# Differential attention scores from rounded parts and remainders, and the modulation's gate row in two parts

## The chip, the cores and the metric

The kernel runs on one core of a Trainium2 chip. The metric is the device time of one execution in microseconds (us), and lower is better. Six actors appear below: PE (TensorE, the matmuls; PEld are its weight loads), ACT (ScalarE), DVE (VectorE), POOL (GpSimd), SP (SyncE, which issues the DMAs here) and the DMA queues. Each engine works through its own instructions in order and waits on semaphores that the others raise.

## The reference, cut to what matters

Two layers run after one another on 1024 tokens of width 1024. The change lies in the second one, in its differential attention, and in a small product that makes the second layer's gate.

```python
# second layer, differential attention: 4 heads, each with two 64-wide halves m = 0, 1
scores_m = (q_m @ k_m.T) * 64 ** -0.5 + alibi_and_causal       # for m = 0, 1
p = softmax(scores_0) - lambda * softmax(scores_1)
o = rms_norm(p @ v) * (1 - lambda_init)                        # then a silu gate
# modulation: shift, scale, gate = split(silu(c) @ ada_w + ada_b)
```

All is float32. TensorE takes plain float32 operands, or operands that were rounded to the type fp32r. A product of full accuracy can also be made from rounded operands: each operand is split into a rounded part (HI) and a remainder (LO), and three products are added up, LO·HI + HI·LO + HI·HI (`PASSES`, line 73). The kernel does that already for all its big projections.

## The kernel before, in words

**The dense run of the second layer.** `Dense` (line 455) computes the projections of the second layer. It goes through *slots*. A slot is one 128x512 half of an output tile: 24 matmuls (8 pieces of depth times 3 passes) into one PSUM bank. The tile's weights are loaded raw, rounded by ACT (`split_high`, line 241) and their remainder is taken by DVE (`split_low`, line 252), one tile ahead. After a slot's matmuls ACT copies the bank to SBUF (a `MapTile`, line 361) and raises `free` for that bank. PE waits for `free` before it writes the same bank again. Slots are numbered from 0 to 51 here; slots 2n and 2n+1 are the two halves of tile n.

**Banks.** The slots 0 to 29 alternate between the banks 7 and 3 (`local`). From slot 30 on, all slots use bank 7 alone (`single`, line 3571), as banks 0 to 3 hold scores by then. So PE can begin slot s+1 only when bank 7 has been emptied of slot s. Slots 20 to 23 make k and q of head 0, slots 30 to 33 of head 1, slots 36 to 39 of head 2, slots 42 to 45 of head 3.

**Work beside the slots.** Other work is interleaved with the slots by hand. Sliding-window attention (`Attention`, scores on line 956, transposes on 967, products with v on 981) goes with the slots 21 to 30. Differential attention (`DiffAttention`, from line 2685) begins after slot 30. It has 32 units (4 heads, 8 blocks of 128 queries); a unit with n blocks of keys has the width 128 n, and n runs 1, 2, ..., 8 in the heads 0 and 2 and 8, ..., 1 in the heads 1 and 3. PE handles them in *bodies*: body u makes the scores of unit u (line 2777), the transposes of unit u-1 (line 2791) and the product with v of unit u-2 (line 2808). There is a body after every slot, and from slot 35 on another one in the middle of every odd slot, after 12 of its 24 matmuls.

**The chain of one unit.** When PE has scored unit u, DVE adds the distances and takes maxima (line 2898), ACT takes exponentials (line 2972), DVE weighs and joins the two halves (lines 2909 to 2913), and PE may then transpose unit u in body u+1.

**Order on DVE in a slot** (`Dense.vector`): first the work of the body in the middle of the slot, then the weights of the unit before (`early_dve`), then `split_low` if the slot is the tile's second half, then the tile's own `vector` (nothing for a `MapTile`), then the maxima of the body after the slot. `split_low` waits for ACT's `split_high`, which in its turn comes after ACT's copy of the slot.

**Row groups.** A score product has a depth of 64. The half m = 0 lies on the partitions 0 to 63 and m = 1 on 64 to 127, and a matmul with 64 rows takes one half of the array's rows. The profile shows a plain float32 matmul as two records of weight load and matmul, and an fp32r one as one.

**Modulation** (line 1795) runs beside the first layer. DVE accumulates silu(c)·ada_w into `acc`; at slot 19 of that run PE sums over the partitions: 16 products of one column (line 1846) and two products of 512 columns with a matrix of ones (line 1849), in plain float32.

## Time and profile before

| what | value |
|---|---|
| median of 3 runs | 1753.31 us (1753.15 to 1753.87) |
| the profiled execution | 1753.49 us, of which the span of its instructions is 1751.8 us |
| PE busy | 1722.8 us, 98% |
| DVE / ACT / POOL busy | 914.2 us (52%) / 653.5 us (37%) / 247.2 us (14%) |
| chain that ended last | 91% PE, 5% DVE, 2% ACT |
| granted TensorE clock | 0.997 of full speed |

The first part of the page says how long each engine had an instruction running, the fourth follows the work that ended last backwards from its end. The timeline of an engine groups neighbouring instructions of one line: start, duration of the group, engine, line, operation, tiles, shapes, count, and in brackets how long the engine had been idle and for whom. Where two groups follow each other closely, the difference of their starts is what the first one cost.

### The profile page before, as it was taken

To read this page: it belongs to the slowest core of one execution; us is meant where nothing else is said; L and a number is where in the kernel's file an instruction comes from. 1 tells how busy PE (TensorE), PEld (TensorE's weight loads), DVE (VectorE), ACT (ScalarE), POOL (GpSimd) and SP (SyncE) were. 2 spreads that over 40 slices of the span, in tenths; PEclk is the share of its full clock that TensorE was granted. 3 is DMA by queue.
4 is the path that set the end of the run, shared out by engine and by line. 5 is a ranking of instruction groups with operands and counts; after the bars stand their busy time and mean duration, and the time that the engine had idled before them with its cause. 6 is when DMAs were issued, how large, how long until landed. Compare 5 with 4: busy or idle time off the path is not lost.

```text
span 1751.8 us, 22440 instructions
## 1 busy us (share of the span) xinstructions
PE 1722.8 (98%) x8731; PEld 1397.1 (80%) x8731; DVE 914.2 (52%) x1529; ACT 653.5 (37%) x1225; POOL 247.2 (14%) x412
## 2 busy tenths in 40 slices
PE   7999999999999999999999999999999999999998
PEld 6788887778888888878888788888887777777786
DVE  5158878664436744863233222477242545757763
ACT  5234438621324433842113111323313453434731
POOL 3012210188901100000000000490000000000000
PEclk9999999999999999999999999999999999999999
DMA  4121110346232200211111211332703101001132
GB/s 146 50 78 41 44 37 2 119 141 196 85 123 72 61 25 28 79 34 50 50 54 39 88 43 30 109 132 79 162 25 101 47 25 37 25 25 49 43 128 107
DMA packets 148485, 122.94 MB, mean 70 GB/s; under 512 B 10572, under 2 KB 134043, under 8 KB 147739
## 3 DMA queue, kind: packets, MB, share of 16 engines
q1 hardware_dynamic: 148378, 121.49, 22.9%
q8 instruction: 70, 1.15, 0.3%
q14 instruction: 37, 0.30, 0.1%
HBM read 108.21 MB, written 13.26 MB: 69 GB/s over the span
## 4 chain that ended last, share of the span: by engine, by line
PE 91%; DVE 5%; ACT 2%; issue 2%; DMA 1%; SPq 0%; DVEq 0%; ACTq 0%
PE psum L91 59%; PE psum L309 8%; PE psum L79 7%; PE psum L981 2%; PE psum L956 2%; PE psum L2777 2%; PE psum L967 2%; PE psum L2808 2%; PE psum L2791 1%; PE psum L1790 1%; PE psum L781 1%; PE psum L1513 1%; ACT p L1085 1%; DVE roots L434 0%; PE psum L415 0%
## 5 line engine op out<-in xcount | busy, mean ns | idle before, releaser
L91 PE MATMUL psum<-hT,w_parts 128*128 128x512 f32 x3360 | 794.2, 392 | 4.0 <-ACT hT L690 2.4
L91 PEld LDWEIGHTS psum<-hT,w_parts 128*128 128x128 f32 x3360 | 627.3, 188 | 140.6 <-issue 5.5
L252 DVE TENSOR_TENSOR w_parts<-w_raw,w_parts 128x1024 fp32r<-128x1024 f32 x88 | 110.3, 1253 | 363.9 <-ACT w_parts L241 363.9
L91 PE MATMUL psum<-h2T,w_parts 128*128 128x512 f32 x1248 | 297.1, 394 | 0.0
L91 PEld LDWEIGHTS psum<-h2T,w_parts 128*128 128x128 f32 x1248 | 230.8, 188 | 48.3 <-issue 1.7
L1548 ACT ACTIVATE gate<-psum,cols 128x512 f32<-128x512 f32 x48 | 33.0, 688 | 284.3 <-PE psum L79 284.3
L79 PE MATMUL psum<-y_high,wp_parts 128*128 128x512 f32 x384 | 128.8, 395 | 0.3 <-DVE ya_low L1606 0.3
L241 ACT CAST w_parts<-w_raw 128x1024 fp32r<-128x1024 f32 x88 | 91.6, 1041 | 21.8 <-DMA w_raw<-w_in 17.2
L79 PEld LDWEIGHTS psum<-y_high,wp_parts 128*128 128x128 f32 x384 | 72.0, 188 | 18.8 <-DVE ya_low L1606 1.6
L309 PE MATMUL psum<-w_parts,y_parts 128*128 128x512 f32 x360 | 82.6, 390 | 0.6 <-DVE w_parts L302 0.6
L434 DVE RECIPROCAL x<-x 128x512 f32<-128x512 f32 x24 | 80.3, 3344 | 0.0
L2972 ACT ACTIVATE diff_p<-diff_p,diff_small 128x128 f32<-128x128 f32 (+7 forms) x64 | 49.2, 770 | 81.1 <-DVE diff_small L2902 81.1
L309 PEld LDWEIGHTS psum<-w_parts,y_parts 128*128 128x128 f32 x360 | 67.3, 188 | 15.1 <-DVE w_parts L302 1.0
L309 PE MATMUL psum<-w_parts,merged_high 128*128 128x512 f32 x240 | 75.9, 392 | 0.0
L1560 DVE TENSOR_TENSOR gate<-psum,gate 128x512 f32<-128x512 f32 x32 | 22.0, 688 | 80.5 <-ACT gate L1548 80.5
L2898 DVE CUSTOM_DVE_ANT_0 diff_p<-psum,far 128x128 f32<-128x128 f32 (+7 forms) x64 | 45.8, 754 | 27.2 <-PE psum L2777 27.0
L2086 POOL MEMSET ssm_cos<- 128x16 f32 x1 | 0.1, 127 | 403.8 <-PE psum L79 403.8
L405 POOL TENSOR_TENSOR sq_parts<-x,sq_parts 128x512 fp32r<-128x512 f32 x24 | 31.0, 1293 | 176.4 <-ACT sq_parts L398 176.4
L309 PEld LDWEIGHTS psum<-w_parts,merged_high 128*128 128x128 f32 x240 | 45.1, 188 | 10.0
L248 DVE TENSOR_TENSOR w_parts<-w_raw,w_parts 128x512 fp32r<-128x512 f32 x32 | 24.5, 792 | 47.2 <-ACT w_parts L237 46.9
L309 PE MATMUL psum<-w_parts,merged_low 128*128 128x512 f32 x112 | 44.0, 393 | 0.0
L1085 ACT ACTIVATE p<-p,att_small 128x128 f32<-128x128 f32 (+1 forms) x96 | 42.1, 439 | 1.9 <-DVE att_small L1023 0.9
(378 smaller groups left out, 2271.2 us busy)
## 6 DMA issues: line engine op xcount, KB each, us to landing
w_raw<-w_in SPq DMA_DIRECT2D x188, 256.0 KB, 3.4
middle_a<-ada_w SPq DMA_DIRECT2D x32, 384.0 KB, 3.8
w_raw<-w_out SPq DMA_DIRECT2D x16, 512.0 KB, 3.8
qkT<-x SPq DMA_DIRECT2D x8, 512.0 KB, 7.0
w_raw<-m_w_kv SPq DMA_DIRECT2D x16, 256.0 KB, 3.2
base<-x SPq DMA_DIRECT2D x8, 512.0 KB, 4.0
x_kept<-x_ring SPq DMA_DIRECT2D x8, 512.0 KB, 3.4
base<-x_kept SPq DMA_DIRECT2D x8, 512.0 KB, 3.5
```

Of the source, the lines that this page charges most:

```text
L79: last = pe.matmul(out, lhs(a, k), rhs(b, k), start=(k == 0 and n == 0), stop=(k == depth - 1 and n == 2))
L91: last = pe.matmul(out, lhs(a, k), rhs(b, k), start=(n == 0), stop=(n == len(SLOT) - 1))
L241: act.copy(self.parts[:, u, HI, :, :], self.raw[:, :, :]).then_inc(self.high, 2)
L252: dve.tensor_tensor(self.parts[:, u, LO, :, :], self.raw[:, :, :], self.parts[:, u, HI, :, :].bitcast(F32), ALU.subtract).then_inc(self.lo ...
L309: last = pe.matmul(out, lhs(a, k), self.part(b, k)[:, c0:c0 + width], start=(i == 0 and n == 0), stop=(i == KT - 1 and n == 2))
L434: dve.reciprocal(rs, rs).then_inc(run.inverted, 1)
L956: last = pe.matmul(self.S_(u)[:, h, 0:d["width"]], d["q"][h], d["k"][h], start=True, stop=True)
L967: last = pe.transpose(self.T_()[:, (2 * h + b) * P:(2 * h + b + 1) * P], self.p[u % self.ring][:, h, b * P:(b + 1) * P], self.ident)
L981: last = pe.matmul(d["out"](h, self.O_(u)), d["values"](h, b), self.pT[u % self.turns][:, (2 * h + b) * P:(2 * h + b + 1) * P], start=(b = ...
L1085: last = act.activation(into, src, ACT.Exp, bias=self.negative[:, s, h:h + 1], accum_out=sums[:, h:h + 1])
L2898: last = dve.tensor_tensor_reduce(self.p[:, s, m, 0:width], bank(self.core, 2 * m)[:, 0:width], self.far[:, D - width:D], 2.0 ** -(5 + h), ...
L2972: last = act.activation(self.p[:, s, m, 0:width], self.p[:, s, m, 0:width], ACT.Exp, bias=self.negative[:, s, m:m + 1], accum_out=self.tot ...
```

## The change

1. q and k of the differential attention are kept as two fp32r parts. Their tiles become `PartsTile`s: ACT writes the rounded part (times the scale), then DVE computes bank·scale − rounded part as one `scalar_tensor_tensor` of 128x512, and DVE, no longer ACT, raises `free`.
2. The scores take three fp32r passes per half m and per chunk of at most 512 columns in place of one plain float32 product.
3. Modulation's gate row: ACT rounds `acc_gate`, DVE takes the remainder in place (both at slot 18), and PE sums both parts with fp32r ones, which the run's head tiles have made already (`same`), in four matmuls in place of two.
4. `diff_q` and `diff_k` take 16 KB more per partition, so the tiles behind them and two of the output norm's tiles move up by 16 KB, and the scratch space for dynamic DMAs is set to 256 bytes to make room.

```diff
+class PartsTile(GateTile):
+    def scalar(self, act, run, s):
+        slot = run.slots[s]
+        wait = self.wait and self.wait(slot.h)
+        if wait:
+            act.wait_ge(*wait)
+        act.activation(self.high(slot.h), run.out(s), ACT.Copy, scale=self.scale).then_inc(run.mapped, 1)
+
+    def vector(self, dve, run, s):
+        slot = run.slots[s]
+        dve.wait_ge(run.mapped, run.gates.index(s) + 1)
+        dve.scalar_tensor_tensor(out=self.low(slot.h), in0=run.out(s), scalar=self.scale,
+                                 in1=self.high(slot.h).bitcast(F32), op0=ALU.mult,
+                                 op1=ALU.subtract).then_inc(run.free[slot.bank], 1)
...
@@ Modulation
+        if s == self.SUM_AT - 1:
+            act.wait_ge(self.weighed, 4 * KT)
+            act.copy(self.high, self.acc_gate).then_inc(self.round_made, 1)
...
+            pe.wait_ge(self.same_made(), 1)
+            pe.wait_ge(self.rest_made, 1)
             for h in range(2):
-                last = pe.matmul(bank(self.core, 5 + h, 1), self.ones,
-                                 self.acc[:, 2 * D + h * HALF:2 * D + (h + 1) * HALF], start=True, stop=True)
+                half = slice(h * HALF, (h + 1) * HALF)
+                pe.matmul(bank(self.core, 5 + h, 1), self.same, self.high[:, half], start=True, stop=False)
+                last = pe.matmul(bank(self.core, 5 + h, 1), self.same, self.low[:, half], start=False, stop=True)
...
+        if s == self.SUM_AT - 1:
+            dve.wait_ge(self.round_made, 1)
+            dve.tensor_tensor(self.low, self.acc_gate, self.high.bitcast(F32), ALU.subtract).then_inc(self.rest_made, 1)
...
@@ DiffAttention.scores
         for c0 in range(0, width, HALF):
             cw = min(HALF, width - c0)
-            for m in range(2):
-                rows = slice(64 * m, 64 * m + 64)
-                last = pe.matmul(bank(self.core, 2 * m)[:, c0:c0 + cw], self.qT[rows, h % 2, t * P:(t + 1) * P],
-                                 self.kT[rows, h % 2, c0:c0 + cw], start=True, stop=True)
+            for n, (a, b) in enumerate(PASSES):
+                for m in range(2):
+                    rows = slice(64 * m, 64 * m + 64)
+                    last = pe.matmul(bank(self.core, 2 * m)[:, c0:c0 + cw], self.qT[rows, h % 2, a, t * P:(t + 1) * P],
+                                     self.kT[rows, h % 2, b, c0:c0 + cw], start=(n == 0), stop=(n == 2))
...
-            qT = core.sb(run_stack, "diff_q", [P, 2, S])
-            kT = core.sb(run_stack, "diff_k", [P, 2, S])
+            qT = core.sb(run_stack, "diff_q", [P, 2, 2, S], F32R)
+            kT = core.sb(run_stack, "diff_k", [P, 2, 2, S], F32R)
...
-                return [MapTile(at(1024, h), ACT.Copy, lambda m: half(kT[:, h % 2, :], m), **where),
-                        MapTile(at(512, h), ACT.Copy, lambda m: half(qT[:, h % 2, :], m),
-                                scale=64 ** -0.5 * 2.0 ** (5 + h), **where),
+                part = lambda a, n: (lambda m: half(a[:, h % 2, n, :], m))
+                return [PartsTile(at(1024, h), part(kT, HI), part(kT, LO), **where),
+                        PartsTile(at(512, h), part(qT, HI), part(qT, LO), scale=64 ** -0.5 * 2.0 ** (5 + h), **where),
...
-    nc = bacc.Bacc("TRN2", target_bir_lowering=False, num_devices=1)
+    nc = bacc.Bacc("TRN2", target_bir_lowering=False, num_devices=1, dynamic_dma_scratch_size=256)
```

On PE, around the bodies 1 and 2 (after the slots 31 and 32), the rows stand before as here (a row is line, operation, output and inputs, shape of the output, count; L2777 are scores, L2791 transposes, L2808 the product with v, L91 a slot):

```order
L2777 MATMUL psum<-diff_k,diff_q 128x256 x2
L2791 MATMUL psum<-const,diff_p 128x128
L91 MATMUL psum<-h2T,w_parts 128x512 x24
L2777 MATMUL psum<-diff_k,diff_q 128x384 x2
L2791 MATMUL psum<-const,diff_p 128x128 x2
```

and with the change, where the lines 2812 and 2826 are the scores and the transposes:

```order
L2812 MATMUL psum<-diff_k,diff_q 128x256 x6
L2826 MATMUL psum<-const,diff_p 128x128
L91 MATMUL psum<-h2T,w_parts 128x512 x24
L2812 MATMUL psum<-diff_k,diff_q 128x384 x6
L2826 MATMUL psum<-const,diff_p 128x128 x2
```

Nothing has moved on PE; each pair of score matmuls has become six.

On DVE, in slot 31 (the second half of head 1's k) and up to the weights of its unit, before (L252 is `split_low`, the ISA rows are the maxima):

```order
L252 TENSOR_TENSOR w_parts<-w_raw,w_parts 128x1024
L2898 ISA diff_p,diff_small<-psum,far 128x256
L2898 ISA diff_small 128x1
L2898 ISA diff_p,diff_small<-psum,far 128x256
L2898 ISA diff_small 128x1
```

and with the change:

```order
L252 TENSOR_TENSOR w_parts<-w_raw,w_parts 128x1024
L398 SCALAR_TENSOR_TENSOR diff_k<-psum,diff_k 128x512
L2933 ISA diff_p,diff_small<-psum,far 128x256
L2933 ISA diff_small 128x1
L2933 ISA diff_p,diff_small<-psum,far 128x256
```

The remainder stands behind `split_low` and ahead of the maxima, and bank 7 is free only after it. All the second halves (slots 21, 23, 31, 33, 37, 39, 43, 45) look like this.

On DVE, in slot 36 (the first half of head 2's k), before (L1531 puts turned v rows away):

```order
L2913 SCALAR_TENSOR_TENSOR diff_p<-diff_p,diff_small 128x896
L1531 COPY diff_v<-psum 128x512
L2898 ISA diff_p,diff_small<-psum,far 128x1024
L2898 ISA diff_small 128x1
L2898 ISA diff_p,diff_small<-psum,far 128x1024
```

and with the change:

```order
L2948 SCALAR_TENSOR_TENSOR diff_p<-diff_p,diff_small 128x896
L1553 COPY diff_v<-psum 128x512
L398 SCALAR_TENSOR_TENSOR diff_k<-psum,diff_k 128x512
L2933 ISA diff_p,diff_small<-psum,far 128x1024
L2933 ISA diff_small 128x1
```

The remainder of a first half stands directly ahead of the maxima of the body after the slot. In slot 36 it waits for an ACT copy which itself waits until unit 7, the last of head 0, has been scored, since head 2's k takes the place of head 0's.

## Rows read from the trace of the kernel before

**Rows 1.** The page, part 1: busy us (share of the span) xinstructions of each engine.

```profile
PE 1722.8 (98%) x8731; PEld 1397.1 (80%) x8731; DVE 914.2 (52%) x1529; ACT 653.5 (37%) x1225; POOL 247.2 (14%) x412
```

**Rows 2.** Groups by form: line, engine, operation, names, shapes, count, busy us, mean ns.

```profile
L91 PE MATMUL psum<-memT,w_parts 128*128 128x256 f32 x192 | 23.9, 280 | 0.4 <-DVE mergedT L436 0.3
...
L2884 DVE SCALAR_TENSOR_TENSOR yT<-psum,diff_norm,yT 128x512 f32<-128x512 f32 x8 | 5.6, 746 | 0.7 <-PE psum L2758 0.7
```

**Rows 3.** Timeline of PE, score bodies with n = 1 and n = 8.

```profile
1439.30 0.49 PE L2777 MATMUL psum<-diff_k,diff_q 64*128 64x128 f32 x4
1439.72 5.75 PE L91 MATMUL psum<-h2T,w_parts 128*128 128x512 f32 x24
...
1487.36 1.99 PE L2777 MATMUL psum<-diff_k,diff_q 64*128 64x512 f32 x8
1489.28 0.98 PE L2791 MATMUL psum<-const,diff_p 128*128 128x128 f32 x7
```

**Rows 4.** Timeline of PE, other matmuls with few rows or few columns.

```profile
57.86 2.10 PE L839 MATMUL psum<-mergedT 33*4 33x384 f32 x6
...
447.76 2.37 PE L1846 MATMUL psum<-const,middle_a 128*128 128x1 f32 x20
449.99 1.96 PE L1849 MATMUL psum<-middle_a,const 128*128 128x512 f32 x4
...
1404.28 1.14 PE L956 MATMUL psum<-wk,wq 64*128 64x256 f32 x8
1405.35 1.09 PE L967 MATMUL psum<-const,swa_p 128*128 128x128 f32 x8
```

**Rows 5.** Timeline of ACT in the slots 31, 32 and 36.

```profile
1445.51 0.60 ACT L361 ACTIVATE diff_k<-psum 128x512 f32<-128x512 f32 x1 [3.93 <-PE psum L91]
1446.00 1.04 ACT L241 CAST w_parts<-w_raw 128x1024 fp32r<-128x1024 f32 x1
...
1452.01 0.60 ACT L361 ACTIVATE diff_q<-psum 128x512 f32<-128x512 f32 x1 [1.47 <-PE psum L91]
...
1489.46 0.60 ACT L361 ACTIVATE diff_k<-psum 128x512 f32<-128x512 f32 x1 [4.21 <-PE psum L2777]
```

**Rows 6.** Timeline of DVE, `split_low` in the slots 31, 33, 39, 43 and 45.

```profile
1447.14 1.23 DVE L252 TENSOR_TENSOR w_parts<-w_raw,w_parts 128x1024 fp32r<-128x1024 f32 x1 [4.67 <-ACT w_parts L241]
...
1460.54 1.23 DVE L252 TENSOR_TENSOR w_parts<-w_raw,w_parts 128x1024 fp32r<-128x1024 f32 x1 [3.92 <-ACT w_parts L241]
...
1526.71 1.23 DVE L252 TENSOR_TENSOR w_parts<-w_raw,w_parts 128x1024 fp32r<-128x1024 f32 x1 [0.57 <-ACT w_parts L241]
...
1562.66 1.23 DVE L252 TENSOR_TENSOR w_parts<-w_raw,w_parts 128x1024 fp32r<-128x1024 f32 x1 [1.73 <-ACT w_parts L241]
...
1579.57 1.23 DVE L252 TENSOR_TENSOR w_parts<-w_raw,w_parts 128x1024 fp32r<-128x1024 f32 x1 [0.65 <-ACT w_parts L241]
```

**Rows 7.** Timeline of PE, the matmuls of the next slot after 31, 32, 33, 39, 43, 45.

```profile
1446.25 5.72 PE L91 MATMUL psum<-h2T,w_parts 128*128 128x512 f32 x24
...
1453.17 5.70 PE L91 MATMUL psum<-h2T,w_parts 128*128 128x512 f32 x24
...
1460.61 5.71 PE L91 MATMUL psum<-h2T,w_parts 128*128 128x512 f32 x24
...
1528.05 5.70 PE L91 MATMUL psum<-h2T,w_parts 128*128 128x512 f32 x24
...
1562.19 5.70 PE L91 MATMUL psum<-h2T,w_parts 128*128 128x512 f32 x24
...
1580.74 5.71 PE L91 MATMUL psum<-h2T,w_parts 128*128 128x512 f32 x24
```

**Rows 8.** Timelines of DVE and PE: maxima and transposes of unit 7.

```profile
1489.40 1.22 DVE L2898 CUSTOM_DVE_ANT_0 diff_p<-psum,far 128x1024 f32<-128x1024 f32 x1 [1.24 <-PE psum L2777]
...
1496.27 1.09 PE L2791 MATMUL psum<-const,diff_p 128*128 128x128 f32 x8
```

**Rows 9.** Timeline of PE: transposes of the window attention's unit 0, after slot 22.

```profile
1371.41 0.66 PE L967 MATMUL psum<-const,swa_p 128*128 128x128 f32 x4
```

25 lines of the change are left out of this document (17 added, 8 removed).

## The prediction

> **What bounds the kernel now.** I read the page's busy times first: PE has an instruction running in 98% of the span [rows 1], so the time changes with what PE executes and with every wait that PE gets. Then I read PE's timeline from slot 30 to the end of the dense run, and beside it those of ACT and DVE, since the change gives DVE new work there. Two things are to be seen. A score body costs its matmuls plus a fixed part. And PE's stretch between two slots is short (0.85 us after slot 31: ACT's copy begins at 1445.51 [rows 5], the next slot at 1446.25 [rows 7]); in it bank 7 must be emptied. A copy of 0.60 us on ACT alone just fits.
>
> **Part 1, the scores.** With n = 1 a body's scores take 1439.72 − 1439.30 = 0.42 us, with n = 8 1489.28 − 1487.36 = 1.92 us [rows 3]: 0.21 + 0.214 n. The slope is 4 columns' time at 2.4 GHz per column of one half m (128 × 4 / 2.4 GHz = 213 ns), so the two halves run side by side. That this comes from the two row groups is seen from two other rows: three plain float32 products that all lie in the first row group take 2.0 us for 384 columns each (six records of 0.32 us, one after another), while four products of 256 columns, two in each group, take 1.07 us, half of what they would one by one, plus 0.21 [rows 4]. The 0.21 us is thus the price of going to 64 rows and back. Over 4 heads and n = 1 to 8 the scores cost 4 × (8 × 0.21 + 36 × 0.214) = 37.5 us.
>
> With the change a chunk takes three passes. No row shows an fp32r matmul of 64 rows. What a pass costs is read from fp32r matmuls of full depth: 24 in 5.7 us, 0.235 us for 512 columns [rows 3, 7], and 23.9 / 192 = 0.125 us for 256 [rows 2], so about 0.02 us beyond the columns. For 128 columns the weight load is the floor: 20 records with one column each lie 2.23 / 20 = 0.11 us apart [rows 4]. I take the two halves as parallel, as they are now, and keep 0.21 us for the switch. Then a unit costs 0.54, 0.59, 0.75, 0.92, 1.25, 1.29, 1.46, 1.62 us for n = 1 to 8 (from n = 5 on it has two chunks), 8.42 us a head and 33.7 in all: **−3.8 us**. It is a small gain since three passes replace four columns' time, and weight loads eat part of it.
>
> The bounds: 23.0 us if passes run at column rate with no switch and no load exposed; 60.7 us if the halves run one after another (53.9 for passes, 6.7 for switches). I choose the parallel value, as its nearest row is the same body in plain float32. The Trainium skill (TensorE: Matmul & The Clock Gate, Part 3, on packing small matmuls) measures four row tiles at 3.07 times, 77% of the ideal; by that as an estimate passes would take 27 / 0.77 = 35 us and the sum would be some 6 us worse after waits. The float32 rows reach the full factor of two, so the sum doesn't use it.
>
> **Part 2, the remainder on DVE before bank 7 is free.** The new instruction reads PSUM and SBUF, 128x512; the nearest row is the `scalar_tensor_tensor` of the same form, 0.75 us long and 0.70 us of DVE's time (5.6 / 8) [rows 2]. The ends are 0.62 and 0.75. In a *second half* DVE does `split_low` first, which waits for ACT's copy and ACT's rounding of the weights. Bank 7 is free 0.75 us after `split_low` gives DVE up (1.14 us after its start) and PE sees it 0.07 us later. The scores ahead are shorter by the amounts of part 1.
> - Slot 31: 1447.14 + 1.14 + 0.82 = 1449.10 [rows 6]; PE would begin at 1446.25 − 0.05 [rows 7]: **2.9 us** of waiting.
> - Slot 33: 1460.54 + 1.96 = 1462.50, against 1460.61 − 0.15: **2.0**.
> - Slot 39: 1526.71 + 1.96 = 1528.67, against 1528.05 − 0.15: **0.8**.
> - Slot 43: 1562.66 + 1.96 = 1564.62, against 1562.19 − 0.10: **2.5**.
> - Slot 45: 1579.57 + 1.96 = 1581.53, against 1580.74 − 0.20: **1.0** [rows 6, 7].
> - Slot 37: nothing. Its body holds scores with n = 7, eight transposes and a product of eight, more than 4 us, and the bank needs some 3.9.
>
> In a *first half* there is no `split_low`: copy 0.60, hand-over 0.10, remainder 0.75, hand-over 0.07, so 1.52 us after the copy begins. Slot 32: 1452.01 + 1.52 = 1453.53 [rows 5] against 1453.17 − 0.10 [rows 7]: 0.45. The slots 30 and 42 miss by about 0.1 each, 44 is even, 36 and 38 have bodies of over 4 us. **0.6 us** together. What is queued on DVE behind the waiting remainder are the maxima of the body after the slot. In the slots with a wait on PE the unit's chain then has PE's whole next slot (5.7 us) as cover.
>
> **Part 3, the maxima of unit 7 come late.** In slot 36 ACT's copy begins only at 1489.46 [rows 5], when unit 7 is scored; the maxima of unit 7 begin at 1489.40 now [rows 8] and would stand behind the remainder, at 1489.46 + 0.60 + 0.08 + 0.70 = 1490.84, 1.44 us later. This chain (maxima, exponentials, weights over 1024 columns) takes until 1496.27, when PE transposes [rows 8]; PE's scores of the next unit end there too, so nothing hides it. With these scores 0.29 us shorter the wait is **1.7 us**.
>
> **Part 4, window attention.** In slot 21 the remainder stands behind `split_low` and ahead of the maxima of its unit 0, whose transposes are already the thing PE waits for at 1371.41 [rows 9]. 0.70 us later: **0.7 us**. The later units have over 1 us to spare. Elsewhere in the run two banks alternate, and a remainder has a whole slot of cover.
>
> **Part 5, gains given back.** At units 11, 22, 25 and 29 and in the last four bodies PE meets a chain of DVE and ACT that is just in time or late; scores that end sooner only wait longer there: **0.5 us** of the 3.8.
>
> **Part 6, the gate row.** Two plain products (four records, 1.8 us without the tail of the last [rows 4]) become four fp32r matmuls of 0.235 us: **−0.85 us**. ACT's rounding (1.04 us, as that of the weights [rows 5]) and DVE's remainder (1.23 us by the form of `split_low`) lie in slot 18, over 3 us ahead of use. Moved addresses and the smaller scratch: every DMA stays in its place on SP; nothing.
>
> **The sum.** Waits 2.9 + 2.0 + 0.8 + 2.5 + 1.0 + 0.6 + 1.7 + 0.7 + 0.5 = 12.7 us; less 3.8 and 0.85: +8.05 us on the profiled execution's 1753.49 (span 1751.8 and 1.7 around it), 1761.5. The median lies 0.2 us below that execution: **1761.3 us**, 0.46% slower.
>
> **The rivals.**
> *A: the two halves don't overlap in fp32r.* For it: no row shows it overlapping. Against: rows 3 and 4, where the row group decides and not the operand. The scores cost 60.7 us, +23.2; each body then covers more, and the waits fall to about 7 (slots 31, 33 and 43 keep 5.8 of 7.4, window attention 0.7, the rest nearly nothing): 1753.3 + 23.2 + 7 − 0.85 = 1782.7.
> *B, the other side: the passes run at column rate.* If going to 64 rows cost nothing in fp32r and the loads hid wholly, the scores would take 23.0 us, −14.5. The waits on bank 7 and on late chains would grow to about 16.5, as every body is shorter by the same amount that PE then stands: 1753.3 − 14.5 + 17.3 (with window attention's 0.7) − 0.85 = 1755.3, within 0.2% of before. It decides from scores under 25 us on. Against it: the 0.21 us appears in every body of 64 rows, whatever n.
> *C: the waits don't come*, since the remainder is not on the way of bank 7, or `split_low` isn't ahead of it: 1753.3 − 3.8 − 0.85 + 2 = 1750.6. Against: the order on DVE and the single bank are written in the program.
> *D: weight loads of the two halves go one after another*, 0.21 us a pass as a floor: 39.1 us of scores, +1.6 instead of −3.8, part of which replaces waits: 1765. It is in my own range.
>
> **How the numbers follow.** The forecast goes from 1757 (switch at half its price, remainder of 0.62 us) over D's 1765 to passes half as dear again (40.5 us for 27, +13.5, of which about 5 replaces waits), 1769: 0.80. A 0.12, B 0.05, C 0.03. The range takes in the forecast and B's bound, 1755.3 to 1769; A stays out with its 0.12. A measurement of this kernel tells 0.2% (3.5 us) from no change. Slower by more: forecast and A, less a little for a low forecast, 0.90. Same: B and that little, 0.07. Faster: C, 0.03.
>
> **What the changed profile would show.** Score bodies: 0.54 us with n = 1, 1.62 with n = 8 (A: 3.0; B: 1.3). Idle time of PE ahead of line 91, released by DVE's line 398: near 2.9, 2.0, 0.8, 2.5, 1.0 us after the slots 31, 33, 39, 43 and 45. A wait of some 1.7 us ahead of the transposes of unit 7. PE's busy time would fall while the span grows. If the bodies are right and the waits are absent, parts 2 to 4 are wrong; if the waits are there and the bodies are long, part 1 is.

## The result and the profile after

| what | before | changed kernel |
|---|---|---|
| median | 1753.54 us (4 runs beside the changed kernel) | 1763.6 us (1762.81 to 1764.69, 4 runs) |
| ratio to before | 1 | 1.0056 (95% interval 1.0044 to 1.0068) |
| the profiled execution, its span | 1753.49 us, 1751.8 us | 1764.33 us, 1762.5 us |
| mean granted TensorE clock | 0.997 | 0.994 |

The change makes the kernel 0.56% slower. Predicted were 1761.3 us and a range of 1755.3 to 1769.0.

The page of the changed kernel, the busy times of part 1 and the chain by engine of part 4:

```profile
PE 1723.5 (98%) x8827; PEld 1408.4 (80%) x8827; DVE 924.6 (52%) x1546; ACT 655.3 (37%) x1226; POOL 250.5 (14%) x412
...
PE 91%; DVE 5%; ACT 2%; issue 2%; DMA 0%; ACTq 0%; DVEq 0%
```

Against [rows 1] PE is busy 0.7 us more, while the prediction had its busy time fall, as its scores became shorter. That was the first sign of something that the prediction doesn't have.

PE's timeline, the score bodies with n = 1 and n = 8 (start, duration of the group, engine, line, operation, tiles, shapes, count, and in brackets the idle time and its releaser), to be held against [rows 3]:

```profile
1440.01 0.55 PE L2812 MATMUL psum<-diff_k,diff_q 64*128 64x128 f32 x6
1440.49 0.73 PE L91 MATMUL psum<-h2T,w_parts 128*128 128x512 f32 x2
...
1494.10 1.66 PE L2812 MATMUL psum<-diff_k,diff_q 64*128 64x512 f32 x12
1495.69 0.98 PE L2826 MATMUL psum<-const,diff_p 128*128 128x128 f32 x7
```

From start to start the scores take 0.48 us with n = 1 and 1.59 with n = 8. Between them are 0.55, 0.72, 0.90, 1.18, 1.25 and 1.42 us: 8.09 us a head, 32.4 in all, against 37.5 before.

PE's timeline, the next slot after 31, 32, 33, 39, 43 and 45, to be held against [rows 7]:

```profile
1449.87 7.33 PE L91 MATMUL psum<-h2T,w_parts 128*128 128x512 f32 x24 [2.84 <-DVE diff_k L398]
1458.61 5.74 PE L91 MATMUL psum<-h2T,w_parts 128*128 128x512 f32 x24
1467.99 5.68 PE L91 MATMUL psum<-h2T,w_parts 128*128 128x512 f32 x24 [1.82 <-DVE diff_q L398]
...
1535.71 5.72 PE L91 MATMUL psum<-h2T,w_parts 128*128 128x512 f32 x24 [0.38 <-DVE diff_q L398]
...
1572.16 7.30 PE L91 MATMUL psum<-h2T,w_parts 128*128 128x512 f32 x24 [2.33 <-DVE diff_k L398]
...
1592.88 5.70 PE L91 MATMUL psum<-h2T,w_parts 128*128 128x512 f32 x24 [0.81 <-DVE diff_q L398]
```

Two things are to be seen. Five of the six have PE idle ahead of them, released by DVE's line 398, the remainder; before, none had. And two of them last 7.3 us for the same 24 matmuls that take 5.7 us elsewhere. PE's clock at these places, in windows of 2 us (window, length, then busy us and instructions of PE, PEld, DVE, ACT and POOL, the granted clock, the DMA share, GB/s):

```profile
1450.00:1452.00 2.00, 2.00 (x6) 1.54 (x7) 0.77 (x7) 1.24 (x5) 0.00 (x0) 0.50 0.77 226
...
1468.00:1470.00 2.00, 2.00 (x9) 1.68 (x10) 1.69 (x7) 0.70 (x2) 0.00 (x0) 1.00 0.72 210
...
1574.00:1576.00 2.00, 2.00 (x6) 1.51 (x6) 1.05 (x3) 0.65 (x3) 0.00 (x0) 0.50 0.26 77
```

Behind the waits of 2.84 and 2.33 us PE ran at 0.50, that is at 1.2 GHz, and did six matmuls in 2 us instead of nine; behind the one of 1.82 us it ran at 2.4 GHz. The half clock counts as busy time: at these two slots alone it adds 3.2 us of it, against some 5 us that the scores save.

How slot 31 goes, in the timelines of ACT and DVE (against [rows 5, 6]):

```profile
1446.26 0.60 ACT L393 ACTIVATE diff_k<-psum 128x512 fp32r<-128x512 f32 x1 [3.92 <-PE psum L91]
```

```profile
1447.89 1.22 DVE L252 TENSOR_TENSOR w_parts<-w_raw,w_parts 128x1024 fp32r<-128x1024 f32 x1 [4.66 <-ACT w_parts L241]
1449.04 0.68 DVE L398 SCALAR_TENSOR_TENSOR diff_k<-psum,diff_k 128x512 fp32r<-128x512 f32 x1
```

The copy is done by 1446.9. The remainder could start then, but DVE's queue has `split_low` first, and this waits for ACT's rounding. The remainder runs from 1449.04, PE goes on at 1449.87.

Unit 7 and window attention: DVE's timeline in slot 36, then PE's ahead of the transposes of unit 7 and around slot 22 (against [rows 8, 9]):

```profile
1496.50 0.69 DVE L398 SCALAR_TENSOR_TENSOR diff_k<-psum,diff_k 128x512 fp32r<-128x512 f32 x1 [1.60 <-ACT diff_k L393]
1497.11 1.21 DVE L2933 CUSTOM_DVE_ANT_0 diff_p<-psum,far 128x1024 f32<-128x1024 f32 x1
```

```profile
1503.97 1.09 PE L2826 MATMUL psum<-const,diff_p 128*128 128x128 f32 x8 [1.61 <-DVE diff_p L2948]
```

```profile
1370.88 1.14 PE L978 MATMUL psum<-wk,wq 64*128 64x256 f32 x8 [0.54 <-ACT swa_p L1107]
```

The wait of unit 7 is where it was forecast. That of window attention stands one step earlier: PE waits 0.54 us ahead of the next unit's scores (line 978, before 956) for ACT's exponentials, and not ahead of the transposes. The trace of before has no idle time at these scores.

### The profile page after: what moved, and what is told of

The parts are those of the page before. It is cut to its first block, busy times and chain, and to the rows that moved or that the text cites. A ratio compares the mean times of both kernels' runs of the same rounds, so it can differ in the third digit from the quotient of the medians.

```text
span 1762.5 us, 22654 instructions
## 1 busy us (share of the span) xinstructions
PE 1723.5 (98%) x8827; PEld 1408.4 (80%) x8827; DVE 924.6 (52%) x1546; ACT 655.3 (37%) x1226; POOL 250.5 (14%) x412
## 4 chain that ended last, share of the span: by engine, by line
PE 91%; DVE 5%; ACT 2%; issue 2%; DMA 0%; ACTq 0%; DVEq 0%
PE psum L91 58%; PE psum L309 10%; PE psum L79 7%; PE psum L978 2%; PE psum L1003 2%; PE psum L989 2%; PE psum L2843 1%; PE psum L2812 1%; PE psum L1812 1%; PE psum L2826 1%; PE psum L1535 1%; ACT w_parts L241 1%; DVE roots L456 0%; PE psum L803 0%; PE psum L437 0%
## 5 line engine op out<-in xcount | busy, mean ns | idle before, releaser
L91 PE MATMUL psum<-hT,w_parts 128*128 128x512 f32 x3360 | 795.3, 393 | 4.1 <-ACT hT L712 3.1
L91 PEld LDWEIGHTS psum<-hT,w_parts 128*128 128x128 f32 x3360 | 628.7, 189 | 140.5 <-issue 4.4
L91 PE MATMUL psum<-h2T,w_parts 128*128 128x512 f32 x1248 | 300.3, 397 | 8.3 <-DVE diff_k L398 5.2
L252 DVE TENSOR_TENSOR w_parts<-w_raw,w_parts 128x1024 fp32r<-128x1024 f32 x88 | 111.2, 1264 | 358.4 <-ACT w_parts L241 358.3
L91 PEld LDWEIGHTS psum<-h2T,w_parts 128*128 128x128 f32 x1248 | 233.1, 190 | 58.4 <-issue 10.7
L446 ACT ACTIVATE x<-psum,const 128x512 f32<-128x512 f32 x24 | 16.5, 689 | 70.2 <-PE psum L438 70.2
```

What stands on the lines that cost most here:

```text
L91: last = pe.matmul(out, lhs(a, k), rhs(b, k), start=(n == 0), stop=(n == len(SLOT) - 1))
L252: dve.tensor_tensor(self.parts[:, u, LO, :, :], self.raw[:, :, :], self.parts[:, u, HI, :, :].bitcast(F32), ALU.subtract).then_inc(self.lo ...
```

## Experiments on the eviction

**DVE takes the remainder first** (e1_remainder_first).

```diff
+            parts = isinstance(self.tiles[slot.n], PartsTile)
+            if parts:
+                self.tiles[slot.n].vector(dve, self, s)
             if slot.last and slot.n + 2 < len(self.tiles):
                 w.split_low(dve, slot.n // 2 + 1, slot.n % 2)
...
-            self.tiles[slot.n].vector(dve, self, s)
+            if not parts:
+                self.tiles[slot.n].vector(dve, self, s)
```

> The changed kernel with one thing else: in a slot of k or q DVE takes the remainder (line 398) ahead of split_low instead of behind it. Theory: what makes PE stand after the slots 31, 33, 39, 43 and 45 is that bank 7 is freed behind split_low. Then the waits fall from 2.84, 1.82, 0.38, 2.33, 0.81 us to about 0.6, 0, 0, 0.4, 0.1, -7.1 us together. If the half clock that PE shows after the two longest waits comes from these waits, its 2 x 1.6 us go too: 1763.6 - 7.1 - 3.2 = 1753.3 us. Rival 1, the clock fell for another reason in these stretches: 1756.5. Rival 2, the bank's release isn't what PE waits for: 1763 and the same waits.

Measured: 1753.87 us (1751.46 to 1755.66, 11 runs), ratio to before 0.9996 (0.9987 to 1.0005). PE's timeline has two waits for line 398 left, and both slots behind them are at full clock:

```profile
1446.12 5.72 PE L91 MATMUL psum<-h2T,w_parts 128*128 128x512 f32 x24 [0.70 <-DVE diff_k L398]
...
1562.04 5.72 PE L91 MATMUL psum<-h2T,w_parts 128*128 128x512 f32 x24 [0.20 <-DVE diff_k L398]
```

One exchange of two instructions on DVE takes away all that the change had cost, some 10 us in the medians. Set beside the changed kernel, start by start, e1 gains 11.1 us from 1370 to 1593 us: 1.6 at each of the two slots that were at half clock, the rest where the waits were. The theory holds, half clock included; both rivals fall.

**The scores alone** (e2_scores_alone), on the kernel before:

```diff
-            for m in range(2):
-                rows = slice(64 * m, 64 * m + 64)
-                last = pe.matmul(bank(self.core, 2 * m)[:, c0:c0 + cw], self.qT[rows, h % 2, t * P:(t + 1) * P],
-                                 self.kT[rows, h % 2, c0:c0 + cw], start=True, stop=True)
+            for n in range(3):
+                for m in range(2):
+                    rows = slice(64 * m, 64 * m + 64)
+                    last = pe.matmul(bank(self.core, 2 * m)[:, c0:c0 + cw], self.qT[rows, h % 2, t * P:(t + 1) * P],
+                                     self.kT[rows, h % 2, c0:c0 + cw], start=(n == 0), stop=(n == 2))
...
-            qT = core.sb(run_stack, "diff_q", [P, 2, S])
+            qT = core.sb(run_stack, "diff_q", [P, 2, S], F32R)
```

> The kernel before, with nothing but the scores changed: ACT writes k and q as fp32r, and each score product is made three times from these same parts (the remainders are left out, so the scores are three times what they should be), with six matmuls a chunk as in the changed kernel. Eviction, order on DVE and gate row are as before. Theory: the bodies' scores cost 32.4 instead of 37.5 us, -5.1, of which about 0.5 comes back at late chains of DVE: 1753.5 - 4.6 = 1748.9 us. Rival: bodies that end sooner only wait longer for DVE and ACT, so little is left: 1752 to 1753.5. Score bodies of 0.48 us with n = 1 and 1.59 with n = 8 in either case.

Measured: 1750.48 us (1748.70 to 1751.88, 11 runs), ratio 0.9979 (0.9970 to 0.9987), 3.3 us less than before beside it. The bodies take 0.48 and 1.59 us, as expected. From 1440 us to the end the trace gains 4.0 us on that of before, so 1.1 of the 5.1 came back as waits, not 0.5, and the median lies between the theory's 1748.9 us and the rival's 1752. No slot has a wait for an eviction. So the scores by themselves are a gain, and it is the eviction that turns the sign.

**The remainder alone** (e3_remainder_alone), on the changed kernel, with the gate row undone too:

```diff
-            for n, (a, b) in enumerate(PASSES):
-                for m in range(2):
-                    rows = slice(64 * m, 64 * m + 64)
...
+            for m in range(2):
+                rows = slice(64 * m, 64 * m + 64)
+                last = pe.matmul(bank(self.core, 2 * m)[:, c0:c0 + cw],
+                                 self.qT[rows, h % 2, HI, t * P:(t + 1) * P].bitcast(F32),
+                                 self.kT[rows, h % 2, HI, c0:c0 + cw].bitcast(F32), start=True, stop=True)
```

> The changed kernel with the scores and the gate row undone: k and q are evicted in two parts (ACT, then DVE behind split_low), but the scores are one plain float32 product of the rounded part (the remainder is left out of them), and the gate row is two plain products. Theory: the waits stay, a little smaller since the bodies ahead are as long as before: 2.8, 1.65, 0.3, 2.2, 0.7 and 0.25 us for slots 31, 33, 39, 43, 45, 32, unit 7 late by 1.4, window attention 0.7: +10.0; with the half clock after the two longest waits +3.2 more: 1766.7 us. Rival 1, without half clock: 1763.5. Rival 2, the waits come from shorter score bodies and not from the eviction: under 1756.

Measured: 1767.7 us (1766.86 to 1769.86, 4 runs), ratio 1.0081 (1.0068 to 1.0095). PE's timeline after the slots 31 and 43:

```profile
1450.84 7.24 PE L91 MATMUL psum<-h2T,w_parts 128*128 128x512 f32 x24 [2.75 <-DVE diff_k L398]
...
1574.92 5.68 PE L91 MATMUL psum<-h2T,w_parts 128*128 128x512 f32 x24 [2.20 <-DVE diff_k L398]
```

The waits are there without the new scores, at the sizes expected (2.75, 1.66, 0.39, 2.20, 0.56 us; 1.27 at unit 7). Only one of the two half clocks came. The median is still 1 us above the expectation. The profiled execution has 1.1 us of difference to that of before already ahead of 1370 us, with a half clock from 266 us on and another at 450 us, on which more below. Whether the other three executions had them isn't known.

**A raw copy frees the bank** (e6_raw_copy), on the changed kernel:

```diff
     def scalar(self, act, run, s):
...
-        act.activation(self.high(slot.h), run.out(s), ACT.Copy, scale=self.scale).then_inc(run.mapped, 1)
+        act.activation(self.raw(slot.h), run.out(s), ACT.Copy,
+                       scale=self.scale).then_inc(run.free[slot.bank], 1)
+
+    def round(self, act, run, s):
+        slot = run.slots[s]
+        act.wait_ge(run.free[slot.bank], slot.prior + 1)
+        act.copy(self.high(slot.h), self.raw(slot.h)).then_inc(run.mapped, 1)
...
+    def rest(self, dve, run, s):
+        slot = run.slots[s]
+        dve.wait_ge(run.mapped, run.gates.index(s) + 1)
+        dve.tensor_tensor(self.low(slot.h), self.raw(slot.h), self.high(slot.h).bitcast(F32),
+                          ALU.subtract).then_inc(run.rested, 1)
```

`raw` is the place of `low`, seen as float32. `round` is called behind `split_high`, `rest` behind the maxima of the body after the slot.

> The changed kernel with another eviction of k and q: ACT copies the bank, scaled and unrounded, into the place of the remainder, and this copy alone raises free (as before the change); behind split_high ACT rounds from there, and DVE subtracts in place, behind the maxima of the body after the slot. Theory: bank 7 is free as early as in the kernel before, no maxima stand behind a remainder, so all of the waits after slots, that of unit 7 (1.6 us) and that of window attention (0.5 us) go, and the scores keep their -5.1 less about 0.5: the time of e2_scores_alone, 1750.0 us, a score body of 1.59 us with n = 8, no wait for line 398 on PE. Rival: ACT's additional 0.5 us a slot ahead of the exponentials comes out in waits ahead of PE's transposes: 1752 us.

Measured: 1750.16 us (1748.56 to 1751.65, 10 runs), ratio 0.9974 (0.9965 to 0.9983). On another chip, as e13_raw_copy_again:

> e6_raw_copy once more, beside the two kernels that differ from it at the modulation alone: 1750.2 us, 0.9974 of the kernel before, if the gain of e6 holds on another chip.

Measured: 1751.02 us (1749.30 to 1753.92, 11 runs), ratio 0.9980 (0.9971 to 0.9989). In the trace of e6 ACT copies and rounds in slot 31, PE starts the next slot at once, and the transposes of unit 7 wait 0.33 us instead of 1.61:

```profile
1446.24 0.60 ACT L394 ACTIVATE diff_k_raw<-psum 128x512 f32<-128x512 f32 x1 [3.73 <-PE psum L91]
1446.74 1.04 ACT L241 CAST w_parts<-w_raw 128x1024 fp32r<-128x1024 f32 x1
1447.67 0.62 ACT L400 CAST diff_k<-diff_k_raw 128x512 fp32r<-128x512 f32 x1
```

```profile
1446.98 1.39 PE L91 MATMUL psum<-h2T,w_parts 128*128 128x512 f32 x5
```

```profile
1495.79 1.09 PE L2840 MATMUL psum<-const,diff_p 128*128 128x128 f32 x8 [0.33 <-DVE diff_p L2962]
```

```profile
1449.90 0.69 DVE L408 TENSOR_TENSOR diff_k<-diff_k_raw,diff_k 128x512 fp32r<-128x512 f32 x1
```

No wait for an eviction is left on PE. DVE's remainder costs the same 0.6 us as before, but nobody waits for it; ACT's additional rounding doesn't show either. This version computes all of the change and is faster than both kernels: 3 to 4 us less than the kernel before, about 13 less than the changed one.

## Experiments on the half clock behind a wait

**The bank held longer** (e7_bank_held), on e1:

```diff
+        for n in range(5 if slot.bank == 7 and slot.last and s >= 30 else 1):
+            if n:
+                run.repeats += 1
+                last.then_inc(run.repeated, 1)
+                dve.wait_ge(run.repeated, run.repeats)
+            last = dve.scalar_tensor_tensor(out=self.low(slot.h), in0=run.out(s), scalar=self.scale,
+                                            in1=self.high(slot.h).bitcast(F32), op0=ALU.mult, op1=ALU.subtract)
+        last.then_inc(run.free[slot.bank], 1)
```

> e1_remainder_first, but in the slots 31, 33, 37, 39, 43 and 45 DVE writes the remainder five times, so that bank 7 is free some 2.7 us later. It measures what a wait on PE does to the clock behind it. From the waits 0.70 and 0.20 us of e1 and those of the changed kernel, PE should stand 3.4 us after slot 31, 2.4 after 33, 0.95 after 39, 2.9 after 43 and 1.4 after 45. Theory: the half clock follows a long wait (2.84, 2.75 and 2.33 us had it behind them so far, 2.20, 1.82 and 1.66 had not), so the slots behind the waits of 3.4, 2.9 and 2.4 us take 7.2 us instead of 5.7, the two others 5.7. Rival: the half clock comes at its own times and has nothing to do with the wait: 5.7 us behind one of the long ones or 7.2 behind a short one. Time about 1753.9 + 11 + 4.5 = 1769.

Measured: 1770.5 us (one run). PE's timeline after the slots 31, 33, 39 and 43:

```profile
1451.37 7.31 PE L91 MATMUL psum<-h2T,w_parts 128*128 128x512 f32 x24 [3.60 <-DVE diff_k L403]
1470.23 5.72 PE L91 MATMUL psum<-h2T,w_parts 128*128 128x512 f32 x24 [2.59 <-DVE diff_q L403]
...
1540.29 5.71 PE L91 MATMUL psum<-h2T,w_parts 128*128 128x512 f32 x24 [1.49 <-DVE diff_q L403]
1577.48 7.28 PE L91 MATMUL psum<-h2T,w_parts 128*128 128x512 f32 x24 [3.10 <-DVE diff_k L403]
```

The waits of 3.60 and 3.10 us have a slot of 7.3 us behind them, that of 2.59 us has not, although the theory wanted it behind all three. After slot 45, 1.80 us, there is none either. So a longer wait does bring the half clock on, at two places that had none in e1, but not every long wait does: the theory holds in part, and the rival's sign, full speed behind one of the long waits, was seen too. The time is 1.5 us above the expected 1769.

**The halves in a row** (e8_halves_in_a_row), on the changed kernel:

```diff
-            for n, (a, b) in enumerate(PASSES):
-                for m in range(2):
-                    rows = slice(64 * m, 64 * m + 64)
+            for m in range(2):
+                rows = slice(64 * m, 64 * m + 64)
+                for n, (a, b) in enumerate(PASSES):
```

> The changed kernel with the six score matmuls of a chunk in another order: three passes of half m = 0, then three of m = 1, in place of m = 0 and m = 1 by turns. Theory: two matmuls run side by side only if they follow each other directly and lie in different row groups, so within a half the passes run one after another and only one of the five transitions overlaps: with n = 8 a body's scores take 2 x 5 x 0.213 + 0.2 = 2.3 to 2.8 us instead of 1.59, all scores some 50 us instead of 32.4, and the time is about 1778 us, less what takes the place of waits (3 to 5 us), so 1773 to 1778. Rival: the hardware overlaps the two halves whatever the order, or they never ran side by side: 1.6 us and the same time as the changed kernel, 1763.6.

Measured: 1768.92 us (one run). What it says of the scores stands in the next section. Of the waits it shows this:

```profile
1451.54 8.52 PE L91 MATMUL psum<-h2T,w_parts 128*128 128x512 f32 x24 [2.83 <-DVE diff_k L398]
1470.86 7.31 PE L91 MATMUL psum<-h2T,w_parts 128*128 128x512 f32 x24 [1.82 <-DVE diff_q L398]
```

The waits are those of the changed kernel, 2.83 and 1.82 us, yet here the second has the half clock behind it as well, and behind the first it lasted longer, 2.8 us lost instead of 1.6. With 2.33 us after slot 43 the third came too. In this trace that is 2.8 us more than in the changed kernel's; the rest of its 4.6 us lies ahead of 1440 us.

So, over the slots of the five traces with such waits (the changed kernel, e1, e3, e7, e8): 3.60, 3.10, 2.84, 2.83, 2.75 and two waits of 2.33 us had the half clock behind them, 2.59, 2.20, 1.80, 1.66, 1.49 and less had not, and 1.82 us once had and once had not. Seven of the nine waits of over 2 us had it behind them, and one of the shorter ones. The length alone doesn't decide between 1.8 and 2.6 us. What else does is open. The Trainium skill (TensorE: Matmul & The Clock Gate, Part 1, What's actually happening) says that a monitor of the engine's recent activity sets the clock to one of two levels and that it runs freely, not in step with the kernel. The traces agree as far as they go: only 0.50 and 1.00 and mixtures of them show, and equal waits end differently.

The traces have a better sample of equal waits than the slots. In the first layer PE waits 1.82 us for DVE at 265 to 267 us in all fourteen traces. In six of them (the changed kernel, e3, e5, e6, e8, e10) the half clock begins within 1.6 us of the end of this wait, in the other eight, that of before among them, it doesn't come. In PE's timeline of the changed kernel and of before, the same eight matmuls:

```profile
265.66 2.09 PE L978 MATMUL psum<-qkT 64*128 64x256 f32 x8 [1.82 <-DVE att_small L1045]
```

```profile
266.69 1.14 PE L956 MATMUL psum<-qkT 64*128 64x256 f32 x8 [1.82 <-DVE att_small L1023]
```

Here it cost the changed kernel 0.95 us against before. e5, which has nothing of the new eviction, has the half clock here too, and e1, which has the eviction, has not, so nothing speaks for this 0.95 us being the change's doing.

## Experiments on the row groups

In e8, the body of unit 7 in PE's timeline:

```profile
1498.64 1.66 PE L2812 MATMUL psum<-diff_k,diff_q 64*128 64x512 f32 x12
1500.23 0.98 PE L2826 MATMUL psum<-const,diff_p 128*128 128x128 f32 x7
```

1.59 us, as in the changed kernel, and so it is for every n. My theory, that two matmuls overlap only if they follow each other in the program, is refuted. Either the halves run side by side in whatever order, or the gain isn't from the row groups.

**Both halves in one row group** (e10_same_rows), on e6:

```diff
                     rows = slice(64 * m, 64 * m + 64)
+                    rows = slice(0, 64)
```

> e6_raw_copy, but all six score matmuls of a chunk take their operands from the partitions 0 to 63, so half m = 1 is computed from the data of m = 0 and the output is not the reference's. Everything else is as in e6. Theory: two matmuls run side by side because they lie in different row groups, in whatever order they are issued; in one row group they run one after another: with n = 8 a body's scores take 12 x 0.213 + 0.2 = 2.8 us instead of 1.58, the scores about 54 us in place of 32, and the time is 1750.2 + 21 = 1771. Rival: the side by side comes from something else (the depth of 64, the two banks): 1.6 us and 1750.

Measured: 1771.84 us (one run). The body of unit 7:

```profile
1490.89 3.01 PE L2827 MATMUL psum<-diff_k,diff_q 64*128 64x512 f32 x12
1493.83 0.87 PE L2841 MATMUL psum<-const,diff_p 128*128 128x128 f32 x6
```

2.94 us instead of 1.59; over n = 1 to 8 the bodies take 0.81, 0.90, 1.26, 1.59, 2.20, 2.30, 2.64 and 2.94 us, 58.6 in all instead of 32.3. It is the row groups. These 58.6 us are also what rival A had priced at 60.7, and 1771 was hit within a microsecond, since nearly nothing waits in this kernel. The Trainium skill (TensorEngine Tiling (Array Packing), Tiling Modes, Key Properties) says that different tiles of the array can execute loads and matmuls in parallel. The two runs agree: 58.6 / 32.3 is a factor of 1.81, and e8 shows it in another order of issue too.

## Experiments on the gate row

The profiled pair shows the opposite of what I had forecast here. PE's timeline of the kernel before, behind the two plain products of [rows 4]:

```profile
451.39 6.01 PE L91 MATMUL psum<-hT,w_parts 128*128 128x512 f32 x24
457.24 1.03 PE L1451 MATMUL psum<-const,middle_b 128*128 128x128 f32 x8
```

and of the changed kernel, with the granted clock of that window:

```profile
449.90 0.77 PE L1880 MATMUL psum<-gate_high,same 128*128 128x512 f32 x1
450.46 0.63 PE L1881 MATMUL psum<-gate_low,same 128*128 128x512 f32 x1
...
451.74 6.39 PE L91 MATMUL psum<-hT,w_parts 128*128 128x512 f32 x24
457.97 1.03 PE L1473 MATMUL psum<-const,middle_b 128*128 128x128 f32 x8
```

```profile
450.00:452.00 2.00, 2.00 (x6) 1.63 (x6) 0.01 (x1) 1.97 (x3) 1.77 (x4) 0.50 0.50 143
```

From the first gate matmul to line 1451 (now 1473) it was 7.25 us (449.99 to 457.24) and is 8.07 (449.90 to 457.97): +0.8 instead of −0.85. The matmuls stand 0.43 us apart and not 0.235.

**The gate row alone** (e5_gate_row_alone), on the kernel before, with the change's own lines in `Modulation` and nothing else of it.

> The kernel before with nothing but the gate row changed: rounded part and remainder at slot 18, four fp32r matmuls at slot 19. Theory 1: the four matmuls take 0.235 us each in place of 0.43, -0.85 us: 1752.7 us. Theory 2, from the trace of the changed kernel, where the granted clock was 0.50 from 450 to 452 us and these matmuls stood 0.43 us apart: the clock falls here and the slot behind starts slow, +0.8: 1754.3 us, with a granted clock of about one half in the 2 us behind the sixteen products of one column.

Measured: 1754.23 us (1751.97 to 1755.15, 11 runs), ratio 1.0002 (0.9993 to 1.0011). Clock 0.50 from 450 to 452 us, 7.97 us for the stretch: theory 2, as far as the profiled run goes. The times can't tell the two theories apart: the interval runs from −1.2 to +1.9 us and takes in both −0.85 and +0.8.

**The four matmuls first** (e9_gate_first), on e5:

```diff
-            for j in range(2 * KT):
-                pe.matmul(bank(self.core, 4, 1)[:, j:j + 1], self.acc[:, j * P:(j + 1) * P],
-                          self.ones[:, 0:1], start=True, stop=True)
...
+            for j in range(2 * KT):
+                last = pe.matmul(bank(self.core, 4, 1)[:, j:j + 1], self.acc[:, j * P:(j + 1) * P],
+                                 self.ones[:, 0:1], start=True, stop=True)
             last.then_inc(self.summed, 1)
```

> e5_gate_row_alone, but with the four gate matmuls ahead of the sixteen products of one column instead of behind them. Theory: it is the sixteen products that the half clock follows. Then the four gate matmuls take 0.235 us each at full clock, and the half clock falls on the slot behind: this slot takes 1.7 us longer, and the time is that of e5, 1754.2 us. Rival 1: with the gate row out of the half clock the time is 0.9 us shorter, 1753.3. Rival 2: the half clock starts ahead of the products and has another cause: the gate matmuls stay 0.43 us apart here too.

Measured: 1754.83 us (1750.60 to 1757.24, 11 runs), ratio 1.0000 (0.9991 to 1.0009). The gate matmuls were 0.24 us apart, at full clock; the products and the slot behind them paid instead, 4.54 us for the products (3.5 at full clock) and 7.72 for the slot:

```profile
446.19 4.68 PE L1858 MATMUL psum<-const,middle_a 128*128 128x1 f32 x32
450.73 7.88 PE L91 MATMUL psum<-hT,w_parts 128*128 128x512 f32 x24
```

So in this trace the half clock began within the sixteen products of one column and stayed for the slot behind them. From the first of these twenty matmuls to line 1451 it took 13.2 us (445.25 to 458.45), against 10.0 in e13 below, whose clock was full (446.81 to 456.80): 3.2 us lost, where I had expected 1.7. The theory holds as to the place, not as to the size, and both rivals fall in this trace.

**The products in three pieces** (e11_columns_spread), on e6:

```diff
...
+    def tensor_lows(self, pe, s):
+        self.columns(pe, s, 0, 5)
+
+    def tensor_mid(self, pe, s):
+        self.columns(pe, s, 5, 10)
+
     def tensor(self, pe, s):
+        self.columns(pe, s, 10, 2 * KT)
```

> e6_raw_copy, but the sixteen products of one column of the modulation stand at three places of slot 19 (five after its eighth matmul, five after its twelfth, six at its end) instead of together at its end. Theory: the half clock at 450 us follows 3.5 us of one-column products in one piece. In pieces of 1.1 to 1.3 us they don't bring it on, the four gate matmuls take 0.235 us each and the slot behind runs at full clock: 1.7 us less than e6, 1748.5 us. Rival: the half clock comes all the same: 1750.2.

Measured: 1749.23 us (1748.12 to 1751.44, 5 runs), ratio 0.9968 (0.9956 to 0.9981), whose interval overlaps those of e6. In its trace the half clock came earlier, behind the first two pieces, and the twelve matmuls of the slot behind these took 4.4 us (444.42 to 448.85). The gate matmuls were at full clock:

```profile
446.00:448.00 2.00, 2.00 (x6) 1.60 (x5) 0.00 (x0) 0.00 (x0) 1.76 (x4) 0.50 0.00 0
```

The theory that pieces don't bring it on is refuted; whether the spreading gains half a microsecond can't be told from five runs.

**The gate row undone** (e12_gate_row_undone), on e6: the gate's lines as in the kernel before.

> e6_raw_copy with the gate row as in the kernel before (two plain float32 products). It gives the gate row's own worth. As I predicted it (four fp32r matmuls at 0.235 us instead of 1.8 us) this kernel should be 0.85 us slower than e6, 1751.0. Against that stands that the half clock falls at this place: where it does, the plain products cost twice as much as well (449.99 to 453.37 us in the trace of e2_scores_alone), so these runs should be some 2.5 us above those of e6, and where it doesn't, 0 to 0.9 above: a median of 1750.5 to 1752.5 and a wider spread.

Measured: 1749.75 us (1749.27 to 1751.74, 7 runs), ratio 0.9973 (0.9962 to 0.9984), beside 1751.02 us (0.9980) for e13 on the same chip. The expected median of 1750.5 to 1752.5 was missed: this kernel is not slower than e6. With this kernel the gate row in two parts is worth nothing that these runs can tell.

What it would be worth at an equal clock the traces do say. In e13 the clock was 1.00 here, as in the trace of before:

```profile
450.30 0.48 PE L1894 MATMUL psum<-gate_high,same 128*128 128x512 f32 x1
...
456.80 1.04 PE L1487 MATMUL psum<-const,middle_b 128*128 128x128 f32 x8
```

At full clock the stretch takes 6.50 us in the new form and 7.25 in the old, −0.75, close to the −0.85 of the prediction. With the half clock it depends on how long this lasts. In the new form the stretch takes 8.0 to 8.1 us in six traces and 9.1 in e7 (449.42 to 458.50), where the half clock lasted twice as long as in these (0.54, 0.50, 0.50 and 0.75 in the windows of 2 us from 448 to 456 us, against 0.98, 0.50, 0.67 and 1.00 in the changed kernel); in the old form it takes 8.9 in e3 (450.68 to 459.61) and 10.1 in e12 and e2 (448.74 to 458.82, 450.59 to 460.66), where it again lasted twice as long. Like against like, the new form is about 0.9 us shorter with the short one and 1.0 with the long one. Of the four traces with the plain gate row (before, e2, e3, e12) three have the half clock here, of the ten with the new one nine. The one trace that I predicted from was the odd one among the four. That the medians don't show even the 0.75 us may be chance (the interval of e5 reaches down to −1.2 us) or mean that the half clock comes more often in the new form. That is open.

## Why the prediction was right or wrong

The time, +10.1 us in the median and +10.8 in the profiled execution, is in the range and on the side that was forecast, and the mechanism is the one named. That the range took it in is in part luck: its upper end was drawn for dearer passes, which didn't come, and not for a half clock, which did. The tally of the profiled executions follows, term by term. What a wait cost is measured from start to start: how much further the changed kernel's trace lies behind that of before after the place than ahead of it. After the slots this is 0.1 to 0.3 us more than the idle time in the brackets, since in the trace the modelled end of one group otherwise lies behind the start of the next.

| step | predicted | measured |
|---|---|---|
| part 1, scores | −3.8 | −5.1 |
| part 2, slots 31, 33, 39, 43, 45 | 2.9, 2.0, 0.8, 2.5, 1.0 | 3.0, 2.1, 0.6, 2.6, 1.1 (idle 2.84, 1.82, 0.38, 2.33, 0.81) |
| part 2, first halves | 0.6 | 0.3 at slot 32, the others not seen |
| part 3, unit 7 | 1.7 | 1.6 |
| part 4, window attention | 0.7 | 0.6 |
| part 5, given back | 0.5 | 0.7 (e2: 1.1) |
| part 6, gate row | −0.85 | +0.8 |
| half clock behind two waits | not in the sum | +3.2 |
| elsewhere, between 460 and 1360 us | 0 | −0.6 |
| elsewhere, ahead of 449 us | 0 | −0.1 (−1.0 at the start, +0.95 at 266 us) |

*Part 1* was right in mechanism, two row groups side by side in fp32r (e10 shows the opposite case), and 1.3 us too dear. The mis-sized term is the body, which costs 0.02 to 0.07 us less than reckoned at every n: with n = 1 0.48 us and not 0.54, with n = 8 1.59 and not 1.62, with n = 5 1.18 and not 1.25. Rivals A, B and D fall with the same rows. The figure of the Trainium skill (TensorE: Matmul & The Clock Gate, Part 3), 3.07 times or 77%, is for four row tiles. My estimate of some 6 us more by it didn't come: with two row groups, e10 against e6 is 1.81 of 2, 91%, with the fixed 0.2 us of the switch inside.

*Parts 2 to 4* hold place by place, but for window attention, where PE waits one step earlier than forecast. All waits together, part 5 included, are 12.5 us for 12.7. In slot 31 the chain reads as I had laid it out: `split_low` begins at 1447.89, gives DVE up at 1449.04 (+1.15), and PE goes on at 1449.87 (+0.83 for the remainder and the hand-over, predicted 0.82). The two parts of these 0.82 us were off against each other: the remainder ends after 0.68 us and not 0.75, and PE goes on 0.15 us behind its end and not 0.07. That the order on DVE makes them is shown by e1, that the scores don't by e3. Rival C falls.

*The step that failed* is one that isn't there. I priced PE's waits at their length, and took the matmuls behind a wait to cost the same as ever. Behind the two longest PE ran at 1.2 GHz, and each slot took 1.6 us longer: 5.7 us of matmuls became 7.3. The trace of before held a hint of the price, at its very start, which I hadn't read for this. A wait of 2.39 us ahead of eight matmuls in PE's timeline, and the windows behind it:

```profile
17.45 2.96 PE L91 MATMUL psum<-hT,w_parts 128*128 128x512 f32 x8 [2.39 <-ACT hT L690]
```

```profile
20.00:22.00 2.00, 1.02 (x3) 0.55 (x3) 1.97 (x3) 0.26 (x2) 0.15 (x1) 0.50 0.55 164
```

It is no clean case: PE had stood still for 6.7 us before its first matmul, and within these 2 us it is busy for 1.02 alone. But it was enough for a bound: nothing, or the half clock behind each wait of over 2 us. In e1 and e6, without the waits, the half clock is gone from these slots, and e7 brings it back at the two places where the wait is over 3 us (not at the one of 2.59).

*Part 6* took its price from a single execution in which the clock happened to stay full. The gain at equal clock was right (0.75 for 0.85), but the place is one at which the clock falls in 12 of 14 traces, and a comparison of two executions there is one of two throws.

*Moved addresses and the smaller scratch*, priced at nothing, can't be seen to cost anything: e1 and e6 have them too and are as fast as or faster than the kernel before. The −0.6 between 460 and 1360 us isn't theirs either, as e2, which has none of them, gains 1.3 us on before there. The greater part of it (0.87 us in both) lies at 1184 us, where the trace of before has a wait of 0.62 us for DVE that the changed kernel's and that of e2 lack.

The sum: the half clock is missing from it with 3.2 us, the gate row is 1.65 us too low, the scores 1.3 too high, the waits 0.2 too high, and elsewhere there are −0.7: 8.05 + 3.2 + 1.65 − 1.3 − 0.2 − 0.7 = 10.7 us, for 10.8 measured. So errors of both signs met, and the median was missed by 2.3 us.

## What to carry to other kernels

When an eviction becomes two steps, free the bank with the first one: copy the bank once, in full precision, and do the rounding and the remainder from SBUF behind work that someone waits for. Where the two steps must both read the bank, look at what stands in the second engine's queue ahead of the second one; here a single exchange was worth 10 us of 1764. Price a wait of the tensor engine above its length where it is over two microseconds or so, by 1.6 us of slower matmuls here, which seven of nine such waits had behind them (look for a long wait anywhere in the trace and for the clock behind it), and don't price a stretch with few columns from one execution.

## What the runs showed of the hardware

- Matmuls of 64 rows on the two row groups ran side by side even when the program issues three of one group and then three of the other: 1.59 us in both orders with n = 8, 2.94 in one group. I had not expected the order to be free. What puts them side by side isn't shown: the records of the trace start in pairs in both orders and don't name the half.
- In the second layer's slots a wait of 2.75 us and more had PE at 1.2 GHz behind it in all five cases, and so had both of 2.33 us; those of 2.59 and 2.20 us had not. Of two waits of 1.82 us one had it, and of fourteen equal ones at 266 us six. The loss in a slot was 1.6 us, in one case 2.8.
- Sixteen products of one column, 3.5 us together, had the half clock in or behind them in 12 of 14 traces, in one piece and in three.
- The same kernel varies by some 4 to 5 us from run to run on one chip (before: 1752.1 to 1757.9 over three chips), with the half clock coming or not at 266 to 274 and 444 to 458 us among what differs between traces. A difference under 2 us can't be read from a pair of executions of this kernel.
